# Two-layer hybrid mixer on one core: when the mixing stage asks for its loads

## The reference

```
for d in range(2):                       # both directions; the second one over flipped tokens
    oa, sa = gla_chunked(q, k, v, log_a[d], init[d])            # 4 heads, linear attention
    ob, sb = gdn_chunked(q, k, v, log_alpha[d], beta[d], init)  # 4 heads, gated delta rule
    o_gla, o_gdn = o_gla + oa, o_gdn + ob
...
# gdn, per chunk of 64 tokens
kk = k k^T;  L = strict(beta * kk * exp(g_i - g_j));  A = I + L      # exp(...): the decays
U = A^-1 (beta v);  W = A^-1 (beta exp(g) k)
delta = U - W S;  o = (q exp(g)) S + (q k^T * decay) delta;  S = a S + k_dec^T delta
```

## Time and profile before

| what | value |
|---|---|
| median of 3 runs | 1659.67 us (1657.52 to 1660.69) |
| the profiled execution: its time, its span | 1664.6 us, 1662.8 us |
| PE busy, of the whole span | 1517.3 us, 91% |
| mixing stage | 541.6 to about 870 us |
| PE busy in it | 267.6 us |
| mean granted clock of PE in it | 0.93 of full |
| DMA share in it, rate | 0.56, 169 GB/s |

### The profile page before, as it was taken

How to read it: one execution, slowest core, us unless ns; L and a number is a source line. 1 busy time by engine, 2 the same in 40 slices (tenths; PEclk the granted TensorE clock), 3 DMA queues, 4 the chain that set the end, 5 groups by cost and what they waited for, 6 DMA issues and landing times. The chain is left out here.

```text
span 1662.8 us, 33993 instructions
## 1 busy us (share of the span) xinstructions
PE 1517.3 (91%) x14508; PEld 1284.8 (77%) x14508; DVE 946.6 (57%) x1330; ACT 745.6 (45%) x1249; POOL 265.5 (16%) x237
## 2 busy tenths in 40 slices
PE   7699999998899697787888997899999999999997
PEld 6488878786798687776777886788888878888885
DVE  4345451475540245555557439455555599988875
ACT  6446253546541444435434215455555554333333
POOL 0001110011110132233223104132222200000000
PEclk9699999998999899999899999999999999999999
DMA  9313332355984466656614311244445586454322
GB/s 325 84 62 107 89 112 63 111 178 162 290 262 143 126 209 188 196 172 206 182 52 164 115 64 63 96 139 142 156 160 164 177 310 253 141 183 161 123 89 102
DMA packets 195736, 254.44 MB, mean 153 GB/s; under 512 B 34525, under 2 KB 127201, under 8 KB 195586
## 3 DMA queue, kind: packets, MB, share of 16 engines
q1 hardware_dynamic: 190002, 234.31, 43.4%
q0 software_dynamic: 5584, 17.95, 3.4%
HBM read 178.17 MB, written 74.05 MB: 152 GB/s over the span
## 5 line engine op out<-in xcount | busy, mean ns | idle before, releaser
L87 PE MATMUL fps<-xh_m,w1r_hi 128*128 128x512 f32 x448 | 176.6, 394 | 11.9 <-ACT s L2562 3.1
L88 PE MATMUL fps<-xl_m,w1r_hi 128*128 128x512 f32 x448 | 175.5, 392 | 0.0
L89 PE MATMUL fps<-xh_m,w1r_lo 128*128 128x512 f32 x448 | 175.3, 391 | 0.0
L87 PE MATMUL fps<-bh,ah 128*128 128x512 f32 x448 | 174.4, 389 | 0.4 <-DVE acc L2891 0.4
L88 PE MATMUL fps<-bl,ah 128*128 128x512 f32 x448 | 174.3, 389 | 0.0
L89 PE MATMUL fps<-bh,al 128*128 128x512 f32 x448 | 174.3, 389 | 0.0
L80 PE MATMUL ps_main<-whi,hhi 128*128 128x256 f32 x416 | 126.8, 305 | 6.5 <-ACT t_sb L879 4.0
L2534 ACT ACTIVATE ah<-araw 128x2048 fp32r<-128x2048 f32 x28 | 53.8, 1921 | 162.6 <-PE fps L89 133.6
L80 PE MATMUL ps_main<-hhi,whi 128*128 128x512 f32 (+1 forms) x336 | 125.6, 374 | 0.0
L81 PE MATMUL ps_main<-wlo,hhi 128*128 128x256 f32 x416 | 122.8, 295 | 0.0
L82 PE MATMUL ps_main<-whi,hlo 128*128 128x256 f32 x416 | 122.7, 295 | 0.0
(11 more groups left out here) (325 smaller groups left out, 3301.0 us busy)
## 6 DMA issues: line engine op xcount, KB each, us to landing
s_hid<-hb SPq DMA_DIRECT2D x112, 256.0 KB, 2.3
araw<-s_hid SPq DMA_DIRECT2D x28, 1024.0 KB, 5.6
room<-in_w_ada SPq DMA_DIRECT2D x32, 512.0 KB, 4.9
w1raw<-in_w_ff SPq DMA_DIRECT2D x16, 1024.0 KB, 5.7
w2b<-in_w_ff SPq DMA_DIRECT2D x16, 1024.0 KB, 9.8
raw<-in_w_in SPq DMA_DIRECT2D x14, 1024.0 KB, 5.3
s_wl<-room SPq DMA_DIRECT2D x24, 512.0 KB, 4.6
wl<-s_wl SPq DMA_DIRECT2D x16, 768.0 KB, 7.2
```

Source lines behind the costliest of these rows:

```text
L87: pe.matmul(out, lhi, rhi, start=start, stop=False, skip_group_check=True)
L88: pe.matmul(out, lhi, rlo, start=False, stop=False, skip_group_check=True)
L89: return pe.matmul(out, llo, rhi, start=False, stop=stop, skip_group_check=True)
```

## The change

It edits SP's order in the mixing stage, and one count on PE. No load is added or dropped, and no engine computes anything else.

- The first loads of the stage: the 8 decay DMAs go ahead of the 2 key DMAs.
- `wl` of a latent step, 1536 KB, was asked for in two DMAs at the end of the step before. Now it comes in three within its own step: entries 0 to 2 when `solve(r, 0)` has run, entry 3 when `update(r, 0)` has run, entries 4 and 5 when `solve(r, 1)` has run.
- `out_weight` moves from the end of a turn to its middle, behind `values`.
- `token_keys` goes ahead of `keys`, and `keys` with `query_decays` now waits until `scores(p, 0)` has run.
- In `linear`, `gqk` goes ahead of `kin`.

```
--- before.py
+++ after.py
@@ -1375,23 +1375,25 @@
                         c = part(d, n)
                         sp.dma_start(ktn[half(c), n], S["kt"][pos(d, s)][half(c)]).then_inc(ld_kt, 16)
 
+            def weights(s, lo, hi):
+                n = s - TC
+                after(sp, sc_ready, 2 * n - (1 if hi <= 3 else 0))
+                sp.dma_start(wl[:, lo:hi], S["wl"][n, :, lo:hi]).then_inc(ld_wl[0 if hi <= 3 else 1], 16)
+
             def linear(s):
-                after(sp, kt_ready, s)
-                sp.dma_start(kin[:], S["kin"][s]).then_inc(ld_kin, 16)
                 if lat(s):
                     n = s - TC
                     after(sp, sc_ready, 2 * n - 1)
                     sp.dma_start(gqk[:], S["gqk"][n]).then_inc(ld_qk, 16)
-                    sp.dma_start(wl[:, 0:3], S["wl"][n, :, 0:3]).then_inc(ld_wl[0], 16)
-                    after(sp, sc_ready, 2 * n)
-                    sp.dma_start(wl[:, 3:6], S["wl"][n, :, 3:6]).then_inc(ld_wl[1], 16)
+                after(sp, kt_ready, s)
+                sp.dma_start(kin[:], S["kin"][s]).then_inc(ld_kin, 16)
                 after(sp, gs_ready[1], s)
                 if lat(s):
                     after(sp, og_ready, s - TC)
                 sp.dma_start(gva[:], S["va"][s].rearrange("p (h n) -> p h n", h=NH)).then_inc(ld_gv, 16)
 
+            decays(0)
             keys(0)
-            decays(0)
             constants(ld_inc, (str_m, "k_str"), (inc_m, "k_inc"))
             constants(ld_lev, (eye, "k_eye"), (lev_m, "k_lev"))
             linear(0)
@@ -1401,23 +1403,33 @@
 
             def step(p, r):
                 if p is not None:
+                    if lat(p):
+                        sp.wait_ge(tr_ready, 2 * r + 1)
+                        weights(p, 0, 3)
                     if p + 1 < NT:
                         decays(p + 1)
+                    if lat(p):
+                        sp.wait_ge(ds_ready, 2 * r + 1)
+                        weights(p, 3, 4)
                     if p:
                         values(p)
+                    if p < KT:
+                        out_weight(p)
+                    if lat(p):
+                        sp.wait_ge(tr_ready, 2 * r + 2)
+                        weights(p, 4, 6)
+                    if p:
+                        token_keys(p)
                     if p + 1 < NT:
+                        if lat(p):
+                            sp.wait_ge(sc_ready, 2 * (p - TC) + 1)
                         keys(p + 1)
                         if lat(p + 1):
                             query_decays(p + 1)
-                    if p:
-                        token_keys(p)
-                    if p + 1 < NT:
                         linear(p + 1)
                     if p == 0:
                         for i, n in enumerate(("gla_norm_g", "gdn_norm_g")):
                             sp.dma_start(ngain[:, i:i + 1], A[n].rearrange("a n -> n a")).then_inc(ld_ngain, 16)
-                    if p < KT:
-                        out_weight(p)
             steps(step)
 
         @block.gpsimd
@@ -1820,7 +1832,7 @@
                 else:
                     pe.wait_ge(acc_step, 7 * (s - TC) + 4)
                     pe.wait_ge(kt_out, s + 1)
-                pe.wait_ge(ld_wl[g], 16 * (s - TC + 1))
+                pe.wait_ge(ld_wl[g], (16, 32)[g] * (s - TC + 1))
                 for e in range(4 if g == 0 else 3):
                     for a in R2:
                         for c in R2:
```

## The result

The changed kernel takes 1669.9 us (median of 13 runs, 1660.85 to 1675.29), the kernel before 1659.67 beside it: ratio 1.007, 95% interval 1.0046 to 1.0094. It is slower by some 10 to 12 us (10.2 between the medians, 11.6 by the ratio). The forecast was 1652.6 us and faster; time and sign are both wrong. The profiled execution took 1670.41 us.

A forecast was written before the change was run, and what follows sets the result against it. PE was taken to lose time in the mixing stage to instruction fetches queued behind loads. Terms -3.0 - 4.5 + 1.0 + 1.0 - 1.2 - 0.4 = -7.1 us took the median 1659.67 to 1652.6 us, range 1642 to 1664.

The forecast's parts named there:

- What bounds the stage: Mixing stage: PE stalls at borders of 256 instructions while packets queue behind loads; 26.3 us of fetch stalls.
- W: At `states` and the start of the next turn: moving `wl` away removes fetch stalls, -3.0 us.
- S: Around `scores(p, 0)`: `wraw` and part of `wl` now share the DMA engines and lengthen fetch stalls, +1.0 us.
- vtn: ACT's wait for `vtn`: one `wl` DMA ahead makes it land later, delaying PE's level 4 in three turns, +1.0 us.
- K: From level 3 to level 4: holding the keys until `scores(p, 0)` has run shrinks fetch stalls, -4.5 us.
- Clock: Low-clock stretches behind the largest gaps of the eight latent turns: one counted as gone, -1.2 us.
- Head: Start of the stage: decays asked for 0.80 us sooner, first masked copy limited by ACT's fill, -0.4 us.
- marks set for a wrong forecast: Profile signs: `scores` issue gaps above 12 us, ACT's `vtn` wait above 8 us, mean clock off by more than 0.02.
- Rival 3: Denser middle delays the fetch at `scores` due between 681 and 686; slower, +5.7 us, 1665.4 us; chance 0.11.
- Rival 2: Fetch stalls only move within the turn, total bytes unchanged; +0.5, about 1660 us; chance 0.22.
- Rival 5: Smaller largest gaps in turns remove six of eight low-clock stretches; -8 on top of -7, 1645 us; chance 0.12.

The follow-up runs named there:

- b_wl: Kernel before with only `wl` moved out of `linear` into the three places of the changed kernel; 1.0066, 1671.71 us.
- b_hold: Kernel before with only the keys held until `scores(p, 0)` has run, `token_keys` ahead of them; 0.9962, 1654.56 us.
- b_hold_wl: Kernel before with the hold of the keys and the `wl` move together, without the edits of `wraw` and of the head; 1.0034.
- b_late_pr: Kernel before with `token_keys` ahead of keys, keys held until `predict(p, 0)`, and `gqk`, `wl` and `gva` asked for behind `states(p)`; 0.9961.
- b_nowl: Kernel before loading `wl` for the first latent step only, so steps 3 to 9 compute wrong results; 0.9963.

## Why the prediction was wrong, step by step

**What bounds the stage: right.** Fetches at borders of 256 instructions stall PE, 60 packets in both stages, and they are stalls of queueing behind loads. The runs that move only loads change the time by -6 to +11 us. The Trainium skill's rule that the sequencer hides the fetch ("Runtime: NRT & Kernel Launch", section "Instruction fetch mechanics") does not hold here: the same block took 4.92 us or 7.09 with more loads ahead of its successor's packet.

**W, -3.0: the removal was sized well, the arrival was not.** At `states` and `turn_system` the gaps fell by 2.6 us in the changed kernel. It took the hold as well: in b_wl, without it, `states` still has 4.2 us of them. With no `wl` at all the kernel gains 6.1, of which W is a part. But I let bytes that arrive elsewhere cost +1.0 (S), and `wl` costs 17 us there against the 6.1 at the end of a turn: moving it alone measured +11.0, where W, S and `vtn` together said -1.0. The failing step is the sentence "A block in the dense parts lasts 4.9 to 6.8 us, gap included": I read one length for all, and never asked how much work each block has at the place that gives up a load and at the place that takes it. The answer is, gaps taken off, 2.4 us ahead of `scores(p, 0)` and 4.9 up to level 1, against 5.6 to 7.6 at the turn's end, and all of these were to be had from the trace of before.

**S, +1.0: wrong in size and in its bound.** "Most of what is added is issued behind the fetch of this place" is true for `scores(p, 0)`, and irrelevant. It is issued ahead of the two fetches that follow. Of the 5.0 us by which the gaps at L1846 grew, 3.9 belong to the later fetch near `scores(p, 1)` (3.07 at 834.11, 0.80 at 799.21), and 1.1 to the fetch at `scores(p, 0)` in one turn, step 6.

**K, -4.5: right alone (-6.3), wrong in the mixture.** In b_hold it came, though by another sum: the gaps at levels and `predict` fell by 10.9 us, from 18.9 to 8.0, and some 8 us came back at `scores`, at `states` and just behind it:

```profile
PE pg L1835 <- issue: 14.2, 13, 3.1
...
PE pd L1750 <- issue: 6.5, 5, 2.5
...
PE pg L1847 <- issue: 4.5, 2, 2.8
```

In b_hold_wl the hold still seems worth 5 us. In the changed kernel `ktn`, `wraw` and two pieces of `wl` stand where the keys stood, so the fetch between level 3 and 4 gains nothing (the gap at 725.67 is 1.94 us, 1.67 before), and the held keys then meet the fetch after it. I had written "the bytes between 682 and 697 do not fall, they rise" and took a third of the gain all the same.

**vtn, +1.0: as forecast**, 2.5 to 3.7 us of ACT's wait; no run isolates what PE lost by it.

**Clock, -1.2: wrong in sign, and the largest term.** 17 us more at the lower level and 8.0 us more of PE's busy time. I had tied one drop of 3.4 us to one large gap in each of eight turns, and counted drops. The profile of before has seven in the latent turns, none in step 9, and two of them are longer (6.8 and 10.2 us). In the turns of steps 5 to 7 of the changed kernel each lasts 10.2 us (6.8, 3.4 and 10.2 before), with a second stall inside the stretch; three further stretches of 3.4 us are new and one is gone. That the second stall is what prolongs it was not tried by itself.

**Head, -0.4: 0.19 us by the rows**, for I did not see that POOL waits for `inc_m`, which no swap of keys and decays moves. Yet alone the swap measured -4.5 us (-7.6 to -1.2) by the ratio; in the changed kernel it measured +3.6 (1.007 with it, 1.0048 without), which is within the noise of two ratios, and on top of b_late_pr it added nothing. The keys' later landing was priced at nothing; PE now waits 5.7 us for the first `kc`, but starts the system's next part no later. What the swap does stays open.

**The rivals.** Two of the marks set for a wrong forecast fired: `scores` above 12 us (14.5) and the clock off by more than 0.02 (0.023 by the time at the lower level). The first is no mark of a slower kernel: b_hold, which is faster, has 14.2. Rival 3 had the right sign at the price of 5.7 us, and the wrong place: it spoke of the fetch due between 681 and 686, and the gap at `scores(p, 0)` there is 1.44 us in the changed kernel, as before:

```profile
687.88 0.34 PE L1846 MATMUL pg<-wl 64*64 64x64 f32 x7 [1.44 <-issue]
```

What was hit in its place is the pair of fetches that comes next. Rival 2, stalls that only move, describes the fetch gaps well (their sum is 34.6 us of "issue" gaps against 32.9), but it put nothing on the clock. Rival 5 (the clock follows) is what happened with its sign turned round; I should have given the clock a chance in both directions. Still open is whether the parts add: hold 0.9962, `wl` 1.0066, head 0.9973 and `wraw` 1.001 multiply to 1.001 against 1.007.

## What to carry to other kernels

Where an in-order engine stalls at borders of its instruction blocks, each block has a slack: its own work minus the time of a fetch. Put large loads where the block that is running has slack (here 4 to 5 us at the end of a turn, 2.4 up to level 1, none ahead of `scores(p, 0)`), and spread a burst only if every place that takes a piece has it. Price a moved load at the place where it arrives, against every fetch in its landing time and not only the next one. And when a change moves short stalls about, compare the busy time of equal instruction counts before blaming waits: the clock may have changed.

## What the runs showed of the hardware

- Where PE stalls for a block, its first instruction runs some 2.5 us behind the start of the 16 KB packet (729.48 to 731.98, 709.7 to 712.21). Over the stalls of all 18 profiles it is 2.2 to 2.9 us in nine of ten, 3.4 at most. The packet starts when PE begins the block before, or later, never a whole block earlier.
- The packet has no precedence: it waited 1 us on empty queues, 3.8 and 4.6 behind loads, 5.8 in step 8.
- SP's own issue of a load is often slower when an instruction packet starts meanwhile. In nine of the profiles one DMA of `kc`, `qc` or `egb` took 0.43 us to issue in the median, and where a packet started meanwhile 1.2 to 2.6 us in 30 of 58 cases. One of them: `egb`, two DMAs, took 1.73 us at 722.86 in the changed kernel, with a q8 packet in 722.90:723.00. In b_late_pr the same two took 0.90:

```profile
720.82 0.90 SPq L1362 DMA_DIRECT2D egb<-s_row  x2
```

- Fewer bytes alone do not raise the clock: b_nowl's stage has a DMA share of 0.47 instead of 0.56, and a clock of 0.93 as the kernel before:

```profile
534.50:859.90 325.40, 267.27 (x7469) 240.04 (x7469) 166.36 (x411) 147.39 (x420) 96.44 (x77) 0.93 0.47 136
```
